# Expert counts loaded once and ahead on TensorE, and the next large expert's window moved behind the last blocks

## What is computed

```
g_sel = jnp.argmax(g_logits, axis=-1)                     # first block: a group of 8 experts, then 2 of them
top_p, top_i = lax.top_k(jax.nn.softmax(e_sel, axis=-1), MOE_TOPK)
hg = (jax.nn.silu(jnp.einsum('td,edf->tef', xt, w_gate[...]))
      * jnp.einsum('td,edf->tef', xt, w_up[...]))
y = y + jnp.einsum('tef,efd->td', hg * wg[..., None], w_down[...])

top_v, top_i = lax.top_k(logits, TOP_K)                   # second block: 2 of 8 experts
for e in range(N_EXPERTS):
    y = y + gates[..., e:e + 1] * swiglu(h, w_gate[e], w_up[e], w_down[e])
```

## Time and profile before

| | |
|---|---|
| median of 3 runs | 2614.45 us (2613.39 to 2617.2) |
| the profiled execution | 2614.12 us, span of its instructions 2612.2 us |
| granted clock of TensorE over the span | 0.952 |
| TensorE matmul busy | 2276.5 us (87%) |
| VectorE, ScalarE busy | 1791.5 us (69%), 1371.7 us (53%) |
| small experts, first layer | about 201 to 484 us |
| small experts, second layer | about 730 to 1012 us |
| large experts | about 1783 to 2587 us |

### The profile page before, as it was taken

The page is one execution under the profiler, slowest core; times in us unless marked ns, Lnnn a source line. Parts: engine busy times, 40 slices in busy tenths (PEclk is TensorE's granted clock), DMA queues, the critical chain, the costliest instruction groups (busy, mean ns, idle before and its releaser), DMA issues.

```text
span 2612.2 us, 43413 instructions
## 1 busy us (share of the span) xinstructions
PE 2276.5 (87%) x16284; PEld 2115.4 (81%) x16284; DVE 1791.5 (69%) x2094; ACT 1371.7 (53%) x1569; POOL 68.7 (3%) x116
## 2 busy tenths in 40 slices
PE   5669999788599996968799896878999999999997
PEld 4458999786499996957699795768898898998996
DVE  3456776546576765776466667637888888888886
ACT  3326565327166553444343344435777777776765
POOL 0010000100100000100000100000000000000000
PEclk9779999999899998989899998988999999999999
DMA  6227999570369995614255461425899999999993
GB/s 222 78 86 279 376 358 362 153 210 1 99 257 361 366 362 186 188 62 145 81 185 186 131 185 64 145 82 200 304 367 338 335 367 336 347 359 336 344 360 133
DMA packets 335559, 609.70 MB, mean 233 GB/s; under 512 B 11024, under 2 KB 266848, under 8 KB 310736
## 3 DMA queue, kind: packets, MB, share of 16 engines
q1 hardware_dynamic: 329696, 590.84, 64.9%
q0 software_dynamic: 5056, 13.23, 2.3%
q10 hardware_dynamic: 560, 2.10, 0.2%
HBM read 605.08 MB, written 1.05 MB: 232 GB/s over the span
## 4 chain that ended last, share of the span: by engine, by line
PE 78%; DVE 12%; ACT 4%; issue 3%; DVEq 2%; POOLq 1%; DMA 0%; ACTq 0%; POOL 0%; PEldq 0%
PE psum L129 17%; PE psum L131 16%; PE psum L130 16%; PE psum L1904 9%; PE psum L1940 9%; PE psum L1928 2%; DVE weight_ring_rounded L116 1%; PE psum L487 1%; DVE h_cf L2775 1%; ACT scores L760 1%; PE psum L2253 1%; PE psum L2446 1%; PE psum L548 1%; PE psum L1617 1%; PE psum L712 1%
## 5 line engine op out<-in xcount | busy, mean ns | idle before, releaser
L1670 DVE TENSOR_TENSOR weight_ring_rounded<-weight_ring,weights_high_rounded 128x2048 fp32r<-128x2048 f32 x264 | 604.3, 2291 | 87.9 <-ACT weights_high_rounded L1665 87.7
L1665 ACT ACTIVATE weights_high_rounded<-weight_ring 128x2048 fp32r<-128x2048 f32 x264 | 505.0, 1915 | 102.4 <-PE psum L131 98.0
L129 PE MATMUL psum<-weights_high_rounded,scores_rounded 128*128 128x256 f32 x1408 | 405.4, 288 | 5.2 <-issue 3.7
L131 PE MATMUL psum<-weights_high_rounded,scores_rounded 128*128 128x256 f32 x1408 | 398.1, 283 | 0.0
L130 PE MATMUL psum<-weight_ring_rounded,scores_rounded 128*128 128x256 f32 x1408 | 397.7, 282 | 0.0
L1998 DVE TENSOR_TENSOR weight_ring_rounded<-weight_ring,weights_high_rounded 128x2048 fp32r<-128x2048 f32 x128 | 292.9, 2292 | 96.9 <-ACT weights_high_rounded L1993 96.9
L129 PEld LDWEIGHTS psum<-weights_high_rounded,scores_rounded 128*128 128x128 f32 x1408 | 269.4, 191 | 10.1 <-issue 5.2
L130 PEld LDWEIGHTS psum<-weight_ring_rounded,scores_rounded 128*128 128x128 f32 x1408 | 269.6, 191 | 3.4
L131 PEld LDWEIGHTS psum<-weights_high_rounded,scores_rounded 128*128 128x128 f32 x1408 | 269.3, 191 | 0.0
L1904 PE MATMUL psum<-weights_high_rounded,scores_rounded 128*128 128x256 f32 x1024 | 262.8, 294 | 2.6 <-DVE weight_ring_rounded L1998 1.4
L131 PE MATMUL psum<-weights_high_rounded,xT_rounded 128*128 128x512 f32 (+3 forms) x688 | 261.0, 379 | 0.0
(11 more groups left out here) (529 smaller groups left out, 4033.1 us busy)
## 6 DMA issues: line engine op xcount, KB each, us to landing
weight_ring<-in_moe_w_gate_dram SPq DMA_DIRECT2D x152, 1024.0 KB, 6.3
weight_ring<-in_moe_w_up_dram SPq DMA_DIRECT2D x152, 1024.0 KB, 8.3
weight_ring<-in_moe_w_down_dram SPq DMA_DIRECT2D x152, 1024.0 KB, 8.3
weight_ring<-in_w_in_dram SPq DMA_DIRECT2D x20, 1024.0 KB, 6.6
weight_ring<-in_ffn_w_gate_dram SPq DMA_DIRECT2D x11, 1024.0 KB, 5.4
weight_ring<-in_ffn_w_up_dram SPq DMA_DIRECT2D x11, 1024.0 KB, 5.3
weight_ring<-in_ffn_w_down_dram SPq DMA_DIRECT2D x11, 1024.0 KB, 4.9
weight_ring<-in_w_out_dram SPq DMA_DIRECT2D x8, 1024.0 KB, 5.1
```

The costliest lines, as they stand in the source:

```text
L129: nc.tensor.matmul(out, lh, rh, start=start, stop=False)
L131: return nc.tensor.matmul(out, ll, rh, start=False, stop=stop)
L1665: self.c.nc.scalar.activation(ring.high(self.s0 + q, 1, SLOT), ring.view(self.p0 + q, 1, SLOT), ACT.Copy).then_inc(ring.high_ready, 1)
L1670: self.c.nc.vector.tensor_tensor(ring.low(self.p0 + q, 1, SLOT), ring.view(self.p0 + q, 1, SLOT), ring.high(self.s0 + q, 1, SLOT).bitcast( ...
```

## The change

Three edits. In `order`, the step `next_window` is taken out of the place ahead of the last `part`. ScalarE now does it behind `part` and the split of the next gate tile, VectorE behind those and behind the copy of its result half. In `SmallExperts.tensor`, TensorE loads the count of an expert once, ahead of its gate product, keeps it in a register, and both branches use it. In `split_streams`, TensorE loads the counts of all 8 large experts ahead of the first one. ScalarE and VectorE load their counts as before.

```diff
@@ order
-    def order(self, split, squash, part, next_split, next_window):
+    def order(self, split, squash, part, next_split):
...
         for j in range(self.chunks):
-            if j == last and next_window:
-                next_window()
             part(j)
             if j == last:
                 next_split(self.gate(0))
@@ scalar
         self.order(lambda q: self.high(act, q, i), squash, part,
-                   lambda q: next_window and self.high(act, q, i + 1), next_window)
+                   lambda q: next_window and self.high(act, q, i + 1))
+        if next_window:
+            next_window()
         act.wait_ge(*self.half(self.half_made, 2 * self.chunks - 1, i))
         nc.scalar.activation(self.rows[:, 0:512], c.psum[:, 4, :], ACT.Copy).then_inc(self.rows_act.sem, 1)
@@ SmallExperts
     def tensor(self, pe):
+        following = None
         for x in range(-1, self.n):
+            count = following
             if x + 1 < self.n:
+                following = self.load_count(pe, x + 1, 0)
                 self.first(pe, x + 1)
             if x >= 0:
                 self.turn(pe, x)
             if x + 1 < self.n:
-                self.by_width(pe, x + 1, 0, lambda: self.second(pe, x + 1), lambda: self.wide_first(pe, x + 1))
+                self.by_width(pe, x + 1, 0, lambda: self.second(pe, x + 1), lambda: self.wide_first(pe, x + 1), following)
             if x >= 0:
-                self.by_width(pe, x, 0, lambda: self.third(pe, x), lambda: self.wide_third(pe, x))
+                self.by_width(pe, x, 0, lambda: self.third(pe, x), lambda: self.wide_third(pe, x), count)
@@ split_streams
         def _(pe):
+            counts = [load_count(pe, e) for e in range(n)]
             for e in range(n):
                 by_width(pe, 0, e, lambda w: way.tensor(pe, e, lambda: pe.wait_ge(*nth(written, e, 0, 0)), spare) if w == narrow
-                         else way.wide_tensor(pe, e, wide_x, spare))
+                         else way.wide_tensor(pe, e, wide_x, spare), counts[e])
```

More of the change, by code:

```diff
@@ L1737, in vector @@
         self.order(lambda q: self.low(dve, q, i), combine, part,
-                   lambda q: next_window and self.low(dve, q, i + 1), next_window)
+                   lambda q: next_window and self.low(dve, q, i + 1))
         self.used(dve, self.p0 + self.down(self.chunks - 1), i)
@@ L1884, in parts, with load_count, by_width @@
         return self.c.ring.high(self.s0 + 2 * x + a, KD, CH), self.c.ring.low(tile, KD, CH)
-    def by_width(self, eng, x, i, small, wide):
-        count = eng.value_load(self.cnt[0:1, bass.ds(x + self.unroll * i, 1)], min_val=0, max_val=TOK)
+    def load_count(self, eng, x, i):
+        return eng.value_load(self.cnt[0:1, bass.ds(x + self.unroll * i, 1)], min_val=0, max_val=TOK)
+    def by_width(self, eng, x, i, small, wide, count=None):
+        if count is None:
+            count = self.load_count(eng, x, i)
         with eng.If(count < self.W + 1):
@@ L2302, in nth, with load_count, by_width @@
         return signal.sem, step * i + (signal.base + 1 + k)
-    def by_width(eng, x, i, body):
-        e = x + unroll * i
-        count = eng.value_load(cnt_i[0:1, bass.ds(e, 1)], min_val=0, max_val=TOK)
+    def load_count(eng, e):
+        return eng.value_load(cnt_i[0:1, bass.ds(e, 1)], min_val=0, max_val=TOK)
+    def by_width(eng, x, i, body, count=None):
+        if count is None:
+            count = load_count(eng, x + unroll * i)
         with eng.If(count < narrow + 1):
```

## The result

The changed kernel took 2602.03 us (median of 7 runs, 2597.93 to 2605.62), the kernel before 2617.89 beside it (7 runs, 2613.39 to 2627.82): a ratio of 0.9935, 95% interval 0.9917 to 0.9953. The forecast was 2605.6 with a range of 2600 to 2612.5, so faster by over 0.2% came true. Side by side the gain is 15.9 us (12.3 to 21.7 by the interval), more than the 8.8 forecast; the absolute time fits better, because the kernel before took 3.4 us more beside it than the 2614.45 that the prediction started from. The profiled executions took 2614.12 and 2602.03 us, their spans 2612.2 and 2600.1.

A forecast was written before the change was run, and what follows sets the result against it. TensorE was taken to bound all three changed stages. Window -7.1, eight large loads +2.0 and small counts -3.7 summed to -8.8 us, from a median of 2614.45 to 2605.6 us, range 2600 to 2612.5.

The forecast's parts named there:

- Window moved, -7.1: Large-expert hand-overs: TensorE starts its last `third` 1.13 us earlier and keeps 1.0; seven hand-overs give -7.1 us.
- some 0.5: Large-expert hand-overs: new TensorE wait of some 0.5 us for VectorE's window line L1704, where "issue" stood.
- The thinnest point: After a large hand-over, VectorE's split of gate(1) ends at 1891.8 for TensorE's need at 1891.9: fits by 0.1 us.
- a sign of being wrong: Large stage: the prediction is wrong if TensorE also waits for the splits of gate(1) or up(1) after a hand-over.
- never for a landing: Large stage: ScalarE waits for TensorE to free a buffer, 98.0 of its 102.4 us, and never for a landing.
- rival 4: Large stage: DMA, share 0.99, is the bound, so the large term is 0 and the time 2610.7 us; chance 0.04.
- Eight loads ahead, +2.0: Ahead of the first large expert: eight count loads outlast the 3.3 us of cover, so TensorE starts later, +2.0 us.
- eight chains of 0.62 to 0.66 us: Ahead of the first large expert: eight count loads with the branch need 5.2 to 5.4 us.
- Small counts, -3.7: Small stages: 0.65 us more cover ahead of `third` gives -7.5, less cover behind it +3.8; net -3.7 us.
- under queued matmuls, never a wait: Small experts: the count load between the transposes and the up product is hidden under queued matmuls and never a wait.
- these come from a jump: Small stages: TensorE's "issue" waits come from a jump over unused wide code lasting 1 to 3.5 us instead of 0.17.
- the draw of the long jumps: Small stages: which jump is long is drawn anew, as the program has 128 rows fewer; bounds -7.5 and +4.

The follow-up runs named there:

- window_between: Changed kernel, but ScalarE makes the next window ahead of its last part again and VectorE directly behind its last part: 2616.0 us, 0.9981 of the kernel before.
- two_loads_moved: Kernel before, small experts only: count for `third` loaded ahead of the gate product, the load for `second` kept in place: 2620.93 us, 0.9996.
- small_alone: Kernel before with only the small experts' edit, one count load ahead of the gate product: 2604.71 us, 0.9942.
- one_load_per_stage: Large experts as before; TensorE loads one count ahead of each small stage for all 32 experts, branches and wide code kept: 2603.68 us, 0.995.
- one_load_at_second: Kernel before, small experts only: one count load per expert, between the transposes and the up product, kept for the down product: 2610.16 us, 0.9961.
- after: The changed kernel with all three edits against the kernel before: 2602.03 us, 0.9935.

## Why the prediction was right, step by step

- **Window moved, -7.1.** Right in mechanism and size: -7.1 alone, seven waits for L1736 of 0.18 us, seven new ones of 0.47 where "some 0.5" was forecast. In the change it measured -6.3; the 0.66 us of the next point are most of the difference.
- **The thinnest point**, the split of gate(1) that "fits by 0.1 us". It fitted at the first five hand-overs and failed at the last two (0.30 and 0.36 us), which the prediction had named as a sign of being wrong. But it failed on ScalarE, whose own sequencer the sum had left out. ScalarE took that tile late:

```profile
2376.52 1.91 ACT L1665 ACTIVATE weights_high_rounded<-weight_ring 128x2048 fp32r<-128x2048 f32 x1 [2.89 <-issue]
```

```profile
2378.46 2.29 DVE L1670 TENSOR_TENSOR weight_ring_rounded<-weight_ring,weights_high_rounded 128x2048 fp32r<-128x2048 f32 x1 [0.69 <-ACT weights_high_rounded L1665]
```

  The transfer was not late: SyncE issued it at 2363.43, and it landed 5.9 us later, at 2369.3, over 7 us before ScalarE began. The issue in SyncE's timeline, and its time to landing in the DMA view:

```profile
2363.43 0.37 SPq L3106 DMA_DIRECT2D weight_ring<-in_moe_w_gate_dram  x1
...
weight_ring<-in_moe_w_gate_dram SPq DMA_DIRECT2D x1, 1024.0 KB, 5.9
```

  What came late is ScalarE's sequencer. These are its branch at the end of the expert's code (L2319) and the load of the next window's offset, which follows it (L2325); first the fifth hand-over, then the sixth:

```profile
L2319 ACTq COMPARE_BRANCH  x1: 33/33/33, 2272.4 to 2272.4; - x1
L2325 ACTq TENSOR_LOAD <-e_off_i x1: 282/282/282, 2272.8 to 2272.8; - x1
...
L2319 ACTq COMPARE_BRANCH  x1: 33/33/33, 2371.3 to 2371.3; - x1
L2325 ACTq TENSOR_LOAD <-e_off_i x1: 282/282/282, 2375.3 to 2375.3; - x1
```

  From the branch to the next instruction 0.4 us passed at the first five hand-overs and 4.0 and 4.6 us at the last two, and the loads behind it took 1.2 and 0.7 us more before the split. It is the same in all 13 traces: ScalarE's jump lasts 2.8 to 4.6 us at these two hand-overs, and the tile had landed 5 to 8 us before its split began. It looks like the long jumps that TensorE has in the small stages. The kernel before has it too (2.50 and 1.62 us of idle time), hidden by TensorE's slack; these 4.1 us are what the earlier trace rows has beside the 98.0 for TensorE. The prediction's "never for a landing" holds, and rival 4, that DMA is the bound, was wrong. In window_between VectorE and TensorE come to gate(1) 0.9 us earlier, ScalarE's jumps last 4.3 and 4.2 us, and the waits grew to 1.1 and 0.5 us. That a fetch of ScalarE's code takes the time would fit, but is not shown, and why only the last two hand-overs have it is open.
- **Eight loads ahead, +2.0.** Right: +2.06, 0.65 us a load, no overlap. (Its "eight chains of 0.62 to 0.66 us" make 5.0 to 5.3 us, not 5.2 to 5.4; measured are 5.2.) By the 200 ns a register of the Trainium skill, page "Runtime: NRT & Kernel Launch", section "Instruction fetch mechanics", the term would have been 0; the trace decides for 0.65 with the two pieces behind the load. That a load at a hand-over is worth nothing beside the moved window was right too (793.1 against 793.9).
- **Small counts, -3.7.** Here the sum came out on the right side partly by luck. The covers were right to the hundredth (1.40 to 2.04, 1.98 to 1.34), but the gain was -10.0, and it is not the gain of that shift: with the shift alone (two_loads_moved) the stages took +1.4. Worked out on that trace's own jumps, the shift is worth some 3.3 us of wait; longer jumps (55.6 us in sum, 52.5 before) and the larger surplus of waits ahead of the gate product took it back. Two parts of the step failed. First, "under queued matmuls, never a wait", of the load between the transposes and the up product, put its removal at nothing. It never shows as a wait, but taking it away gave 12.7 us (two_loads_moved to small_alone). Second, the price of a wait was taken as the wait that the view shows, without the 0.15 to 0.25 us of slow start behind it; that is the smaller part. And "these come from a jump" holds for 12 of the 17 waits.
- What the prediction called the draw of the long jumps mattered less than feared: moved by 128 instructions the stages differ by 1.0 us, and over five kernels with the load in this place by 4.6.
- **Still open:** why the load at `second` makes long jumps behind `third` longer. With it their sum is 20 to 26 us in six traces, without it 12 to 17 in six, and the two groups don't touch. The loads are not needed for long jumps as such: one_load_per_stage has 49 us of them. A later start of a fetch would fit, but no view shows when one starts.

## What to carry to other kernels

A sequencer's load that never shows as a wait can still cost, through the jumps behind it: test it by removing it, since neither the waits nor the queue's cover priced it. Of three edits that land together, run each alone: here one gave 10 us, one 7, and one took 2, and putting its work in the middle of an expert gave the 2 back. A term that comes out with the right sign is not yet right: give the mechanism a run of its own, as two_loads_moved did here. And a wait marked "issue" ahead of a tile's first use looks like a late transfer, but it can be the sequencer: compare the landing with the branch and the loads ahead of the instruction. Here the tile had lain ready for 7 us, and ScalarE's late jumps are what the next improvement meets.

## What was not expected of the hardware

- A count load on TensorE's sequencer takes 0.30 + 0.15 + 0.02 us in its three instructions, but in a row of eight one begins only every 0.65 us.
- Queued matmuls cover 2.04 us of a jump ahead of the down product and 1.98 ahead of the gate product, 0.64 less where a count load follows the jump, the same to 0.06 us in twelve traces.
- A jump over never-used code lasts up to 3.9 us on TensorE (window_between, 0.17 usually) and up to 4.6 on ScalarE (after, 0.4 at the other hand-overs). On TensorE the wait that it leaves costs 0.15 us (ahead of the down product) to 0.25 us (ahead of the gate product) more than its length.
- Two kernels with the same length of code, and long jumps mostly at the same places, had 43 and 63 us of them, according to where the count load stood (small_alone, one_load_at_second).
